# Loading w1 and w3 of the last four experts as whole 2 MB tensors in a mixture-of-experts trunk

## What is computed

```python
hid = jax.nn.silu(jnp.einsum('td,edf->tef', t, w1)) * jnp.einsum('td,edf->tef', t, w3)
hid = hid * gates[..., None].astype(hid.dtype)
out = jnp.einsum('tef,efd->td', hid, w2)
```

## Time and profile before

| | us |
|---|---|
| median of three runs | 1701.23 |
| the profiled execution, its own time | 1700.64 |
| its span in the trace | 1698.9 |
| PE busy | 1543.7 (91%) |
| VectorE busy | 747.0 (44%) |
| all weight loads of SP's queue | 542.16 MB, 81.4% of 16 DMA engines' span |
| mean granted TensorE clock | 0.957 of full speed |

### The profile page before, as it was taken

One profiled execution on the slowest core, in us unless ns is written; L12 is line 12 of the kernel. 1 busy time (PEld: TensorE's weight loads), 2 busy tenths in 40 slices (PEclk: granted clock), 3 DMA queues, 4 the chain that ended last, 5 costly groups with the idle time before them and its releaser, 6 DMA issues.

```text
span 1698.9 us, 24085 instructions
## 1 busy us (share of the span) xinstructions
PE 1543.7 (91%) x9334; PEld 1028.2 (61%) x9334; DVE 747.0 (44%) x1271; ACT 436.5 (26%) x608; POOL 55.4 (3%) x73
## 2 busy tenths in 40 slices
PE   9999999999997787878899999999999987787875
PEld 9888888788543243323387888888874443233322
DVE  5565655544442222323374757556434323222324
ACT  6344343443100000000255434344320000000002
POOL 0010100100000000000022100000000000000000
PEclk9999999999998998988999999999999989888899
DMA  8655555579999999999965465566899999999998
GB/s 271 212 160 169 166 173 187 211 295 346 393 428 429 431 431 431 431 432 427 406 212 156 150 221 173 173 236 216 315 345 423 428 431 431 432 432 431 431 426 315
DMA packets 149794, 543.87 MB, mean 320 GB/s; under 512 B 15600, under 2 KB 60832, under 8 KB 121952
## 3 DMA queue, kind: packets, MB, share of 16 engines
q1 hardware_dynamic: 140384, 542.16, 81.4%
q10 hardware_dynamic: 9040, 0.49, 0.3%
q0 software_dynamic: 304, 0.31, 0.1%
HBM read 540.83 MB, written 2.10 MB: 320 GB/s over the span
## 4 chain that ended last, share of the span: by engine, by line
PE 68%; DMA 25%; DVE 2%; SPq 2%; ACT 1%; issue 1%; DVEq 0%; ACTq 0%
PE psum_G L896 32%; DMA all_places<-in_moe_w 25%; PE psum_S L896 22%; PE psum_A L896 9%; PE psum_T L896 4%; SPq L670 2%; DVE w_lo L501 1%; ACT w_hi L497 1%; DMA x<-in_x 0%; ACT arena L1549 0%; PE psum_A L903 0%; DVE h L2506 0%; PE psum_T L1179 0%; SPq L620 0%; PE psum_A L942 0%
## 5 line engine op out<-in xcount | busy, mean ns | idle before, releaser
L501 DVE TENSOR_TENSOR w_lo<-ring,w_hi 128x2048 fp32r<-128x2048 f32 x125 | 286.9, 2298 | 261.5 <-ACT w_hi L497 260.4
L896 PE MATMUL psum_A<-all_places,arena 128*32 128x512 f32 x1984 | 269.0, 671 | 78.8 <-DMA all_places<-in_moe_w 75.9
L497 ACT CAST w_hi<-ring 128x2048 fp32r<-128x2048 f32 x126 | 240.1, 1908 | 235.6 <-PE psum_G L896 128.8
L896 PEld LDWEIGHTS psum_A<-all_places,arena 128*32 128x32 f32 x1984 | 60.0, 116 | 215.1 <-issue 185.7
L2389 DVE TENSOR_TENSOR x<-x,psum_S 128x512 f32<-128x512 f32 (+1 forms) x132 | 88.4, 671 | 214.4 <-PE psum_S L896 214.3
L896 PE MATMUL psum_G<-all_places,arena 128*32 128x512 f32 (+1 forms) x1056 | 134.7, 654 | 50.9 <-DMA all_places<-in_moe_w 48.6
L896 PE MATMUL psum_G<-w_hi,xT_pair 128*128 128x512 f32 x512 | 161.2, 391 | 0.0
L2216 DVE COPY arena<-psum_A 128x512 f32<-128x512 f32 x54 | 37.4, 692 | 252.9 <-PE psum_A L896 247.3
L896 PE MATMUL psum_S<-xT_pair,w_hi 128*128 128x512 f32 (+1 forms) x448 | 139.3, 369 | 0.0
L896 PE MATMUL psum_G<-xT_pair,w_hi 128*128 128x512 f32 (+1 forms) x448 | 134.7, 370 | 0.6 <-DVEq L1943 0.6
L896 PE MATMUL psum_S<-arena 128*128 128x512 f32 (+1 forms) x264 | 125.6, 604 | 3.3 <-ACT arena L1804 2.8
(11 more groups left out here) (266 smaller groups left out, 1921.2 us busy)
## 6 DMA issues: line engine op xcount, KB each, us to landing
all_places<-in_moe_w SPq DMA_DIRECT2D x120, 2048.0 KB, 23.9
all_places<-in_moe_w SPq DMA_DIRECT2D x144, 1024.0 KB, 12.1
ring<-in_ml_w_in SPq DMA_DIRECT2D x48, 1024.0 KB, 5.1
ring<-in_sb_w_in SPq DMA_DIRECT2D x47, 1024.0 KB, 5.0
ring<-in_sb_w_out SPq DMA_DIRECT2D x16, 1024.0 KB, 5.0
ring<-in_ml_w_out SPq DMA_DIRECT2D x16, 1024.0 KB, 5.1
x<-in_x SPq DMA_DIRECT2D x4, 512.0 KB, 7.9
out_x<-h SPq DMA_DIRECT2D x3, 512.0 KB, 2.7
```

What stands on the lines that cost most here:

```text
L497: act.copy(w_hi[:, slot_place(j), :], ring[:, slot_place(j), :]).then_inc(hi_made, 1)
L501: dve.tensor_tensor(w_lo[:, slot_place(j), :], ring[:, slot_place(j), :], w_hi[:, slot_place(j), :].bitcast(F32), ALU.subtract).then_inc(l ...
L896: return pe.matmul(dst, lhsT, rhs, start=start, stop=stop, skip_group_check=True)
```

## The change

The last quad loads w1 and w3 of an expert whole, as the middle quads do: 8 transfers of 2 MB in place of 16 of 1 MB, into pairs of neighbouring places. The order of places is new (`LAST_PLACES`, `LAST_STARTS`); w2 pieces keep their sizes but go to other places. SP's waits stand ahead of j = 4 in place of 2, and of 12, 18 and 22 in place of 12, 16 and 20. On PE half 0 of an expert waits for both whole tensors, and half 1 for nothing. `whole_ups` is true for quads 2 to 7, `whole_rows` still for 2 to 6.

```diff
-LAST_PLACES = 2 * [0, 1, 5, 8, 6, 9, 7, 10, 3, 15, 20, 4]
+LAST_PLACES = [0, 8, 1, 9, 6, 10, 7, 11, 2, 4, 3, 5, 0, 8, 1, 9, 15, 20, 6, 7, 10, 11, 3, 4]
+LAST_STARTS = [j for j in range(6 * QUAD) if j >= 4 * QUAD or j % 4 < 2]
...
+        def whole_ups(i):
+
+            return not (isinstance(i, int) and i < 2)
...
-            former = layer * (first + second + NMIDDLE * middle + LAST_PLACES.count(n))
+            former = layer * (first + second + NMIDDLE * middle + sum(1 for m in LAST_STARTS if LAST_PLACES[m] == n))
...
-            return 16 * (former + earlier + places_of(i)[:j + 1].count(n))
+            starts = LAST_STARTS if i == NQUAD - 1 else range(6 * QUAD)
+            return 16 * (former + earlier + sum(1 for m in starts if m <= j and places_of(i)[m] == n))
...
-                if j < 4 * QUAD and whole_rows(i):
+                if j < 4 * QUAD and whole_ups(i):
...
-                for j in range(6 * QUAD):
-                    if j == 2:
+                for j in LAST_STARTS:
+                    if j == 4:
                         sp_eng.wait_ge(*up_done(layer, i - 1, QUAD - 1))
                     elif j == 8:
                         sp_eng.wait_ge(*down_done(layer, i - 1, 1))
-                    elif j in (12, 16, 20):
-                        sp_eng.wait_ge(*up_done(layer, i, j // 4 - 3))
+                    elif j in (12, 18, 22):
+                        sp_eng.wait_ge(*up_done(layer, i, {12: 0, 18: 1, 22: 2}[j]))
...
-                    if half == 0 or not whole_rows(i):
+                    if half == 0 or not whole_ups(i):
                         wait_slot(4 * q + 2 * half)
                         wait_slot(4 * q + 2 * half + 1)
```

## The result

The changed kernel takes 1709.54 us (median of five runs, 1707.62 to 1713.10), the kernel before 1701.23 us beside it. The ratio is 1.0051, 95% interval 1.0040 to 1.0062: slower by 8.3 us. The forecast was 1709.3 us with a range of 1704.4 to 1714.1.

The account below looks back on a forecast made before the run. The stream of weights sets the last quad's pace. Layer 0: 3.9 - 0.3 - 0.3 = 3.3 us; layer 1: 3.9 + 1.6 - 0.3 - 0.4 = 4.8; together 8.1 later, 1709.3 us, range 1704.4 to 1714.1.

Parts of the forecast that it names:

- Where PE starts: Last quad: q3's half 0, folding of q2 and dummies now stand behind the last landing, 3.90 us later in each layer.
- The rate: Last quad's w1 and w3 loads: 2 MB transfers land the last one 0.3 us earlier per layer, at most 0.73.
- SP's waits: Last quad's load queue: moved waits leave no hole, since several loads are always under way; cost nothing.
- What catches it up: Behind the hidden values: waits for w2 parts absorb 0.29 us in layer 0 and 0.42 us in layer 1.
- The clock: Last quad's q3 in layer 1: a 3.0 us wait drops PE to the lower clock, costing 1.6 us; none in layer 0.
- a rival: PE's clock in both layers falls more often or for longer, through halves, dummies and folding: up to 1714.1 us; chance 0.22.
- The checks in the profile: Last quad: waits of 4 and 3 us before half 0, none at half 1, first w2 part 3.3 to 5.2 us later.
- one sign that the prediction named against itself: Last quad: half 0 of q3 starting without a wait would show the prediction wrong; no size given.

Follow-up runs that it names:

- the wide dummies: Changed kernel with 512-column dummy matmuls, 3 ahead of q2 and 4 ahead of q3, in place of 0 and 6 narrow ones: 1710.09 us, ratio 1.0048.
- The wait alone: Kernel before, loads untouched; in the last quad half 0 of an expert waits for all four of its loads, half 1 for none: 1709.76 us, ratio 1.0053.
- q2 and q3 by tensor: Changed kernel, loads untouched; PE takes q2 and q3 of the last quad first with all w1, then all w3, each pass awaiting its own tensor: 1700.57 us, 0.9995.
- the kernel with more dummies: Changed kernel with 10 dummy matmuls ahead of q2 and 16 in place of 6 ahead of q3 of the last quad: 1711.82 us, ratio 1.0069.
- with q3 by tensor: Changed kernel, loads untouched; PE takes only q3 of the last quad first with all w1, then all w3: 1704.76 us, ratio 1.0021.

## Why the prediction was right

**Where PE starts** (3.90 us a layer): right. The term itself measures 3.84 us from half 0 to half 1 of q3 in layer 0 (828.23 to 832.07). In the ten layers of the table in which the clock stayed up at q3 the first w2 part comes 2.9 to 4.2 us later, 3.6 in the mean; the prediction has 3.9 less 0.3. Without the three in which something else held q3 up beyond its landing (q2's clock in layer 0 of the first row, the dummies in layer 1 of the first and third rows of the wide dummies) the mean is 3.4. The wait alone reproduces the loss, and PE's order alone takes it away.

**The rate** (0.3 us a layer): small, as forecast. From the quad 6 down step to the start that q3's last load releases it is 40.36 and 40.52 us before the change (827.23 and 1663.52) and 39.97 in layer 1 after it (1667.56 - 1627.59); in layer 0 no start waits for that landing. With whole loads the runs give 40.37 (second profile of the changed kernel, layer 0, 827.43) to 39.39 (third, layer 0, 826.21). It is a gain of 0 to 1 us, and the sum's 0.3 us lies in it. The wait alone, with its 1 MB loads, gives 40.05 and 40.35, so how much of this comes from the size of the loads is not shown. The fixed cost of each transfer in the Trainium skill (SBUF — State Buffer, The DMA setup-cost knee) would return some 16 us a layer, an estimate from that page; nothing of that size came back. The share of the DMA engines in this stretch is 1.01 before and 1.00 after, so there was no idle time between transfers to win back.

**SP's waits** (nothing): right for this kernel. With them and the new places in force, the kernel with q2 and q3 by tensor is at 0.9995. The lead is not endless: in the kernel with more dummies the wait for q0 ended some 6 us late in layer 1 and left the hole told above.

**What catches it up** (0.3 and 0.4 us): right in size. In layer 1 the 12.1 us by which the first w2 part is later than before (1681.33 against 1669.19) are 11.7 at the last parts (1694.96 against 1683.30). In layer 0 the fourth part no longer waits, and 4.8 us at the first w2 part (837.75 against 832.91) are 4.6 at the next projection (857.51 against 852.93); the rest moved as a whole, and quad 6 of layer 1 starts 4.6 us later too.

**The clock** (1.6 us, in layer 1 alone): the mechanism was right, the term mis-sized. A fall at q2 was hidden by the wait for q3 in three of the four layers where it happened and up to some 0.8 us in the fourth, layer 0 of the profiled run: the prediction had q2 lose 1.6 us there and q3 wait 1.7, but q2 lost 4.2 (8.94 against 4.78) and used the whole wait up. Where the clock falls at q3, in one layer of each of these four profiles, q3 takes 8.0 to 10.2 us from half 0 to the end of half 1 in place of 5.8, and the layers lose 6.1 to 7.8 us in place of 3.6: 2.5 to 4.2 us for the clock. The 1.6 us came from the middle quad, where the lower level ended within the expert; here it lasted, in three of the four, through half 0, folding, dummies and part of half 1, which the prediction had as part of a rival. That it would be layer 1 held in two profiles of the three, and no run shows what chooses the layer.

Nor does the length of the wait, by which the prediction chose, tell when the clock falls: q2 kept it after waits of 2.48, 2.86 and 3.75 us and lost it after 2.02, 2.77, 3.58 and 3.78. The Trainium skill (TensorE: Matmul & The Clock Gate, HAM oscillation) has the clock fall back at every slice whose matmuls are shorter than the wait for the next slice's load. The prediction carried this over to q3 too readily: an expert's up steps take 4.8 us, and of all these waits only the one of 5.01 us is longer, so these profiles neither bear the rule out nor speak against it.

**The checks in the profile.** The waits (3.58 us ahead of q2 in layer 0, 3.42 ahead of q3 in layer 1), the missing wait at half 1, the rate (425 and 426 GB/s) and the vanished waits for w2 came as written. From half 0 of q3 to the end of half 1 it is 5.8 us in layer 0, as forecast, and 10.0 in layer 1, where 7.6 were forecast; the 3.3 to 5.2 us for the first w2 part held in layer 0 (4.0) and not in layer 1 (7.5). And one sign that the prediction named against itself did come: half 0 of q3 in layer 0 started without a wait, because q2 was slower than forecast and not because the load was early.

**The number.** By the measured terms a run with both falls at q2 would take 1701.2 + 2 x 3.6 - 0.7 = 1707.7 us and one with a fall at q3 in one layer some 3.6 us more, 1711.3 (the means of the table, less the slack of 0.3 and 0.4 us behind the first w2 parts). The median, 1709.5, lies between. That the point forecast came within 0.3 us of it is luck: its clock term was less than half of what a fall at q3 costs. How often the clock falls at q3 in runs without a profile stays open.

## What to carry to other kernels

Where a stream of loads sets the pace and the queue is never empty, a larger transfer buys little (here at most 1 us a layer), but it makes the consumer wait for all of it: what counts is the work that is left behind the last landing. Ask of each merged wait which work was done while the second piece was under way; if the consumer can be ordered by piece (here first all of w1, then all of w3), large transfers and early starts go together. A longer wait on TensorE can also cost twice: here once as order, in every layer, and once as clock, in the layers where the fall met work that no later wait hid.

## What the runs showed that was not expected

Kernels with longer waits have more uncertain times. The runs of the kernel with q2 and q3 in halves (1700.45 to 1702.49) lie 2 us apart, those of the kernel before at most 4 (1699.97 to 1703.81, 21 runs), those of kernels with a wait of some 3 us or more 5 to 8 us (the changed kernel 5.5; q3 in halves 7.9, 1699.60 to 1707.46). The profiles show one reason: it changes from run to run which of q2, q3 and the first w2 part meets the lower clock. It isn't the whole reason, since the wide dummies, with waits of at most 1.5 us, spread over 6.6 us.

PE stops at q0 of the last quad in layer 1 with its loads landed: for 1.96 us before the change, 1.51 after it, 6.30 with the 20 more dummies, 5.77 with q3 by tensor, not at all with q2 and q3 by tensor. It never showed in layer 0. It comes behind the loop over the middle quads, and its length differs from kernel to kernel; its cause was not tried. The traces give a hint: in each of the twelve profiles that have the stop a packet of 16 KB on the instruction queue starts, and PE goes on 2.2 to 2.6 us after it (1646.47 and 1649.08 with more dummies, 1643.33 and 1645.78 before the change). The stop also stands at the same instruction in all three profiles of a kernel, and at another one in most kernels whose program is longer or shorter. That points at the loading of PE's program. It isn't shown: no run moved only that, and such packets come without a stop too, in layer 0 and with q2 and q3 by tensor.
